# Activation rows placed 64 bytes ahead of the weight rows modulo 256 in a two-block transformer kernel

## The chip, the cores and the metric

The kernel runs on one core of a Trainium2 chip. Its time is device time in microseconds of one launch: 1126.99 us, the median of three runs (1125.65 to 1127.13).

The engines: TensorE (PE) multiplies, its weight loads are listed apart (PEld); VectorE (DVE), ScalarE (ACT) and GpSimd (POOL) do the elementwise work; SyncE (SP) issues the DMAs. PE reads both operands from the on-chip memory SBUF, 128 partitions wide, and writes into PSUM.

## The reference

Two transformer blocks on 256 tokens of width 1024, all in float32. Cut to what matters:

```python
# first block
h = h + 0.5 * swiglu(rmsnorm(h), w_gate, w_up, w_down)        # 1024 -> 2816 -> 1024
n = rmsnorm(h); z = n @ w_in                                  # q, k, v, u, v_gate
attn = causal_attention(q, k, v)                              # 8 heads of 64
gm   = u * (tril(w_s) @ layernorm(gelu(v_gate)) + b_s)        # chunks of 128 tokens
gates = sigmoid(n @ w_gate + b_gate)
h = h + (gates_a * (attn @ w_branch_attn) + gates_g * (gm @ w_branch_gmlp)) @ w_out
h = h + 0.5 * swiglu(rmsnorm(h), ...)
x = rmsnorm(h)
# second block, on 16 meta tokens + 256 tokens = 272
u = rms_norm(h); proj = u @ w_in
y_a = hgrn2_mixer(q, f, i, g) @ w_hg_o      # S_t = diag(f_t) S_{t-1} + k_t v_t^T, o_t = S_t^T q_t
y_b = mla_mixer(c_q, c_kv, k_pe) @ w_mla_o  # latent attention with rope, 8 heads
h = h + rms_norm((gate_a * y_a + gate_b * y_b) @ w_out)
h = h + rms_norm((silu(gt) * up) @ w_ffn_out)
return h[:, 16:, :]
```

## The kernel before

Features lie on partitions and tokens in the columns. A weight matrix is streamed as 168 slabs of up to 1 MB, 2048 float32 words on every partition, through a ring of three places (`RING`, `SLAB`). `stage` receives a slab by DMA. ACT copies it into `w_hi` in the reduced format fp32r (`split_hi`, L1038), DVE writes the rest `stage - w_hi` into `w_lo` (`split_lo`, L1194). Activations are split in the same way into a high and a low part. `x_hi` and `x_lo` hold eight rows (one for each 128 features) of 272 columns: 16 meta tokens and 256 tokens. `a_hi` and `a_lo` hold eight rows of 256.

`products` (L1372) makes one product of two split operands from three matmuls: w_lo with x_hi, w_hi with x_lo, w_hi with x_hi (L1374 to L1376). The first operand is the stationary one, loaded as 128 columns; the second is streamed, 256 or 272 columns wide. Each matmul comes with a load of its own, which PE does beside the matmul before it.

Which operands `products` gets depends on the slab:

- A feature slab (`feature_slab`, L1381) has 8 x 256 columns of weights, stationary in tiles of 128. It streams row k of x or a, for two outputs, k from 0 to 7: 48 matmuls, the row changes every three matmuls. It reads x from column 16 on (`x_hi[:, :, X0:]`). Nine slabs and one half slab of the second mixer (`FULL`, `one_chunk_slab`) read all 272 columns.
- A down slab (`down_slab`, L1423) has 2 x 1024 columns of weights and streams two rows of the hidden activation, 24 matmuls on the first and then 24 on the second (L1429, the last slab of a block interleaves them). `hidden_part` (L185) says where the hidden rows lie: in the first feed-forward block in rows of a, in the second and third in x rows 4 and 5, or 6 and 7, in turn.
- A token slab (`token_slab`, L1518; four in the first mixer) streams the weights past a stationary x. Branch slabs and the slabs of the latent attention work on a.

The program is five stages: feed-forward on x, first mixer, feed-forward on a, second mixer, feed-forward on a. Each engine's instructions stand in a written order, and semaphores tie them. A feed-forward block runs gate, up and down slabs in turn. The mixers put attention, the gating and the decay levels of the recurrence between slabs. At a level (`level`, L639 on DVE and L1703 on PE) PE multiplies 16 pairs of q and k blocks, and DVE copies those elements into `AT` which the level's mask keeps: eight `copy_predicated` (L684) for each of eight levels.

`sb` (L125) gives each tensor the next free bytes of every partition, in the order of the calls. `stage`, `w_hi` and `w_lo` take 24,576 bytes each, then come `x_hi`, `x_lo` (8 x 1088 bytes each), `a_hi`, `a_lo` (8 x 1024), `h`, `sq`, `ar` (all the mixers' scratch), `tab` (mask, cosines, sines and the level masks `lvl`, 128 columns for each of eight levels), `ident` and small things.

Of the kernel before, what the change touches and what calls it, by code (L numbers as in the profile page):

```python
# [20 lines left out]
F32 = mybir.dt.float32  # L21
F32R = mybir.dt.float32r
# [4 lines left out]
P = 128  # L27
D = 1024
DC = D // P
SEQ = 256  # L30
META = 16
L2 = SEQ + META
X0 = META
FF = 2816
PAIRS = FF // 256
# [13 lines left out]
LEVELS = [0, 1, 2, 4, 8, 16, 32, 64]  # L49
# [22 lines left out]


T_MASK, T_COS, T_SIN, T_LVL = 0, L2, 2 * L2, 3 * L2
TAB = T_LVL + P * len(LEVELS)
NEG = -1e30


def constants():


    tab = np.zeros((P, TAB), np.float32)
    q, k = np.arange(P)[:, None], np.arange(P)[None, :]
    tab[:, T_MASK + L2 - P:T_MASK + L2] = np.where(k <= q, 0.0, NEG)
    inv_freq = (1.0 / (np.float32(10000.0) ** (np.arange(0, ROPE, 2, dtype=np.float32) / np.float32(ROPE)))).astype(np.float32)
    ang = (np.arange(L2, dtype=np.float32)[:, None] * inv_freq[None, :]).astype(np.float32)
    row = np.arange(P)
    sign = np.where(row % ROPE < ROPE // 2, -1.0, 1.0).astype(np.float32)
    tab[:, T_COS:T_COS + L2] = np.cos(ang).T[row % (ROPE // 2)]
    tab[:, T_SIN:T_SIN + L2] = np.sin(ang).T[row % (ROPE // 2)] * sign[:, None]  # L90
    s, t = np.arange(P)[:, None], np.arange(P)[None, :]
    for i, h in enumerate(LEVELS):
        keep = (s == t) if h == 0 else ((s // (2 * h) == t // (2 * h)) & (s % (2 * h) < h) & (t % (2 * h) >= h))
        tab[:, T_LVL + P * i:T_LVL + P * i + P] = keep
    return tab


# [24 lines left out]
def program(nc, a, vec_d, id_d, tab_d, out):  # L122
    ctx = ExitStack()
    with ctx:
        def sb(name, shape, dt):  # L125
            return ctx.enter_context(nc.sbuf_tensor(name, shape, dt))

        s = {}
# [6 lines left out]
        stage = sb("stage", [P, RING, SLAB], F32)  # L135
        w_hi = sb("w_hi", [P, RING, SLAB], F32R)
        w_lo = sb("w_lo", [P, RING, SLAB], F32R)
        x_hi = sb("x_hi", [P, DC, L2], F32R)
        x_lo = sb("x_lo", [P, DC, L2], F32R)
        a_hi = sb("a_hi", [P, DC, SEQ], F32R)  # L140
        a_lo = sb("a_lo", [P, DC, SEQ], F32R)
        h = sb("h", [P, DC, SEQ], F32)
        sq = sb("sq", [P, DC, SEQ], F32)
        ar = sb("ar", [P, 17408], F32)
        tab = sb("tab", [P, TAB], F32)
        ident = sb("ident", [P, P], F32)
# [3 lines left out]
        ones = sb("ones", [P, P], F32)  # L150
        eps = sb("eps", [P, 1], F32)
        pick = sb("pick", [P, 2 * HH - 1], F32)
        warm = sb("warm", [P, 16], F32)
        ss = sb("ss", [P, 2, L2], F32)
        std = sb("std", [P, 2, L2], F32)
        rstd = sb("rstd", [P, 2, L2], F32)
        rcol = sb("rcol", [P, 2, 8], F32)

        mask = tab[:, T_MASK:T_MASK + L2]
        lvl = tab[:, T_LVL:].bitcast(mybir.dt.int32).rearrange("p (l t) -> p l t", t=P)  # L160

        def view(at, *dims):
            n = int(np.prod(dims))
# [39 lines left out]
        tA, tB = view(0, 1024), view(1024, 1024)  # L203
        tC, tD = view(11264, 1024), view(12288, 1024)
        meta = sb("meta", [P, 2, DC, META], F32)
        small = sb("small", [P, 96], F32)

        out_tok = view(2048, NT, D)

# [8 lines left out]
        AT = view(13824, HH, 3, P)  # L218
# [375 lines left out]
        def mixer2_dve(dve, split_lo, seq, inverse, input_lo):  # L594
# [44 lines left out]
            def level(l):  # L639


                size = LEVELS[l]
# [31 lines left out]
                    dve.wait_ge(s["lvl_done"], 4 * l)  # L674
                for b in range(4):
                    for hd in range(2):
                        o, m = AT[:, 2 * b + hd, 0:3:2, :], lvl[:, l, :]
                        d = ps[:, 4 + b, SEQ * hd:SEQ * hd + SEQ].rearrange("p (t q) -> p t q", t=2)
                        if size:
                            o, d = (v.rearrange("p t (b two s) -> p t b two s", two=2, s=size)[:, :, :, 1, :] for v in (o, d))  # L680
                            m = m.rearrange("p (b two s) -> p b two s", two=2, s=size)[:, :, 1, :].unsqueeze(1).to_broadcast([P, 2, P // (2 * size), size])
                        else:
                            m = m.unsqueeze(1).to_broadcast([P, 2, P])
                        op = nc.vector.copy_predicated(o, m, d)  # L684
                    op.then_inc(s["lvl_done"], 1)

# [1231 lines left out]
```

## Time and profile before

| | |
|---|---|
| median of 3 runs | 1126.99 us (1125.65 to 1127.13) |
| profiled execution, from first to last instruction | 1125.5 us |
| PE busy | 1098.5 us, 98% |
| PE weight loads busy | 1067.5 us, 95% |
| DVE, ACT, POOL busy | 699.7 (62%), 516.0 (46%), 93.6 us (8%) |
| matmuls recorded | 8807 |
| bytes moved by DMA | 180.19 MB, 160 GB/s on average |

The times come from one profiled execution. A matmul's duration in a row is its way through a pipeline in which several are under way, so the sum of durations is longer than the time they take. How fast they follow each other is seen in the start times of the timeline (first column, in us from the span's start), or in a stretch's length over the count in brackets. PEclk is the share of PE's full clock of 2.4 GHz that was granted; 0.5 is its lower level of 1.2 GHz.

### The profile page before, as it was taken

Reading aid. Unit: us, or ns where it says so; the run is one execution under the profiler, and the core shown is the slowest. Engines: PE = TensorE matmul, PEld = TensorE weight load, DVE = VectorE, ACT = ScalarE, POOL = GpSimd, SP = SyncE. Lnnn points to the kernel's source line nnn. Section 1 sums busy time; section 2 is a strip of 40 time slices with the busy share of each in tenths; the row PEclk is TensorE's granted clock in tenths of the full one; section 3 lists DMA queues with packets and bytes.
Section 4 is the critical chain, followed back from the end, with each engine's and each line's share of the span. In section 5 each row is a group of like instructions: output and inputs, shape, how many; then the busy total and the mean of one; then the engine's idle time right before and its main releaser. Section 6 shows DMA issues by size and latency. Waiting matters only on the chain.

```text
span 1125.5 us, 20359 instructions
## 1 busy us (share of the span) xinstructions
PE 1098.5 (98%) x8807; PEld 1067.5 (95%) x8807; DVE 699.7 (62%) x698; ACT 516.0 (46%) x558; POOL 93.6 (8%) x90
## 2 busy tenths in 40 slices
PE   6999999999999999999999999999999989999997
PEld 5999999999999999999989888999979989999997
DVE  4755555666858665555689666676636656655552
ACT  5543343535755553343375555322333555444334
POOL 3000000100201200000025700000000021000001
PEclk8999999999999999999999999989998989999999
DMA  8466555465354465555436432423323454555541
GB/s 283 141 224 224 181 189 189 138 199 187 115 185 159 151 215 186 188 185 186 149 109 220 149 113 75 143 84 113 113 85 117 137 187 134 209 196 170 186 149 38
DMA packets 147192, 180.19 MB, mean 160 GB/s; under 512 B 3965, under 2 KB 134258, under 8 KB 147138
## 3 DMA queue, kind: packets, MB, share of 16 engines
q1 hardware_dynamic: 146464, 177.55, 48.3%
q0 software_dynamic: 400, 1.73, 0.5%
q8 instruction: 42, 0.69, 0.2%
q10 hardware_dynamic: 274, 0.13, 0.0%
q14 instruction: 12, 0.10, 0.0%
HBM read 178.34 MB, written 1.05 MB: 159 GB/s over the span
## 4 chain that ended last, share of the span: by engine, by line
PE 93%; DVE 3%; issue 2%; ACT 1%; POOL 1%; DVEq 0%; POOLq 0%; ACTq 0%
PE ps L1374 28%; PE ps L1376 27%; PE ps L1375 27%; PE ps L1720 2%; DVE w_lo L1194 1%; PE ps L1678 1%; PE ps L1677 1%; ACT w_hi L1038 1%; PE ps L1759 0%; PE ps L1700 0%; POOL ss L932 0%; PE ps L1757 0%; PE ps L1842 0%; PE ps L1698 0%; PE ps L1738 0%
## 5 line engine op out<-in xcount | busy, mean ns | idle before, releaser
L1194 DVE TENSOR_TENSOR w_lo<-stage,w_hi 128x2048 fp32r<-128x2048 f32 (+1 forms) x165 | 381.4, 2315 | 213.3 <-ACT w_hi L1038 212.9
L1374 PE MATMUL ps<-x_hi,w_lo 128*128 128x256 f32 (+1 forms) x1480 | 422.9, 286 | 4.7 <-DVE ar L703 2.0
L1376 PE MATMUL ps<-x_hi,w_hi 128*128 128x256 f32 (+1 forms) x1480 | 419.6, 284 | 0.0
L1375 PE MATMUL ps<-x_lo,w_hi 128*128 128x256 f32 (+1 forms) x1480 | 419.5, 283 | 0.0
L1038 ACT ACTIVATE w_hi<-stage 128x2048 fp32r<-128x2048 f32 (+1 forms) x165 | 313.2, 1902 | 222.5 <-PE ps L1376 222.5
L1374 PE MATMUL ps<-a_hi,w_lo 128*128 128x256 f32 (+1 forms) x1112 | 316.9, 285 | 2.8 <-DVE a_lo L1200 2.3
L1376 PE MATMUL ps<-a_hi,w_hi 128*128 128x256 f32 (+1 forms) x1112 | 315.8, 284 | 0.0
L1375 PE MATMUL ps<-a_lo,w_hi 128*128 128x256 f32 (+1 forms) x1112 | 315.8, 284 | 0.0
L1374 PEld LDWEIGHTS ps<-x_hi,w_lo 128*128 128x128 f32 x1480 | 282.9, 191 | 10.8 <-issue 7.5
L1376 PEld LDWEIGHTS ps<-x_hi,w_hi 128*128 128x128 f32 x1480 | 282.7, 191 | 0.0
L1375 PEld LDWEIGHTS ps<-x_lo,w_hi 128*128 128x128 f32 x1480 | 282.0, 191 | 0.0
L1374 PEld LDWEIGHTS ps<-a_hi,w_lo 128*128 128x128 f32 x1112 | 214.4, 193 | 3.5 <-issue 3.0
L1375 PEld LDWEIGHTS ps<-a_lo,w_hi 128*128 128x128 f32 x1112 | 214.6, 193 | 0.1
L1376 PEld LDWEIGHTS ps<-a_hi,w_hi 128*128 128x128 f32 x1112 | 214.4, 193 | 0.0
L1065 ACT ACTIVATE ar<-ar 128x512 f32<-128x512 f32 x33 | 20.8, 631 | 121.5 <-DVE ar L1217 121.5
L928 POOL TENSOR_TENSOR ss<-sq 128x256 f32<-128x256 f32 x7 | 6.5, 925 | 759.7 <-ACT sq L1041 391.3
L1074 ACT ACTIVATE x_hi<-ar 128x512 fp32r<-128x512 f32 x22 | 13.9, 632 | 86.6 <-DVE ar L1229 86.6
L1217 DVE TENSOR_TENSOR ar<-ps,rstd 128x512 f32<-128x512 f32 x33 | 22.8, 690 | 34.4 <-PE ps L1376 34.3
L932 POOL TENSOR_TENSOR ss<-ss,sq 128x256 f32<-128x256 f32 x36 | 31.4, 871 | 28.8 <-ACT sq L1041 18.0
L1720 PE MATMUL ps<-ar 128*128 128x64 f32 (+1 forms) x256 | 30.5, 278 | 1.1 <-DVE ar L684 1.1
L1720 PEld LDWEIGHTS ps<-ar 128*128 128x128 f32 x256 | 30.1, 196 | 1.3 <-issue 1.3
L1074 ACT ACTIVATE a_hi<-ar 128x512 fp32r<-128x512 f32 x11 | 6.9, 632 | 45.8 <-DVE ar L1229 45.8
(292 smaller groups left out, 846.8 us busy)
## 6 DMA issues: line engine op xcount, KB each, us to landing
stage<-in_w_in_dram SPq DMA_DIRECT2D x36, 1024.0 KB, 5.2
stage<-in_ffn_w_up_dram SPq DMA_DIRECT2D x22, 1024.0 KB, 5.4
stage<-in_ffn_w_down_dram SPq DMA_DIRECT2D x22, 1024.0 KB, 5.0
stage<-in_w_ffn_in_dram SPq DMA_DIRECT2D x22, 1024.0 KB, 5.0
stage<-in_ffn_w_gate_dram SPq DMA_DIRECT2D x21, 1024.0 KB, 5.3
stage<-in_w_ffn_out_dram SPq DMA_DIRECT2D x11, 1024.0 KB, 4.9
stage<-in_w_gate_dram SPq DMA_DIRECT2D x8, 1024.0 KB, 5.5
stage<-in_w_out_dram SPq DMA_DIRECT2D x8, 1024.0 KB, 5.1
```

Source lines behind the costliest of these rows:

```text
L932: last = nc.gpsimd.tensor_tensor(dst, dst, src[:, c, :], ALU.add)
L1038: nc.scalar.activation(o, i, ACT.Copy).then_inc(s["hi_ready"], 1)
L1065: nc.scalar.activation(ga_a, ga_s, ACT.Silu).then_inc(s["silu_done"], 1)
L1074: nc.scalar.activation(hidden_part(f, 0, J), pair(hid), ACT.Copy).then_inc(s["hid_hi_done"], 1)
L1194: nc.vector.tensor_tensor(o, i, b.bitcast(F32), ALU.subtract).then_inc(s["lo_ready"], 1)
L1217: nc.vector.tensor_tensor(pair(ga_s), ps[:, g0:g0 + 2, 0:SEQ] if first else pair(ps[:, J % 2, :]), bc2, ALU.mult).then_inc(s["gate_scaled" ...
L1374: nc.tensor.matmul(o, wl, xh, start=start, stop=False, skip_group_check=skip)
L1375: nc.tensor.matmul(o, wh, xl, start=False, stop=False, skip_group_check=skip)
L1376: return nc.tensor.matmul(o, wh, xh, start=False, stop=stop, skip_group_check=skip)
L1677: nc.tensor.matmul(o, qn[:, hd, t:t + P], kn[:, hd, 0:nk], start=True, stop=False)
L1678: last = nc.tensor.matmul(o, q_pe[r:r + ROPE, p, t:t + P], k_pe[r:r + ROPE, 0:nk], start=False, stop=True)
L1720: last = nc.tensor.matmul(o, k2[:, hd, X0 + P * t:X0 + P * t + P], q, start=True, stop=True)
```

## The change

The rows of `x_hi` and `x_lo` are allocated 320 columns wide (`X_ROW`), 1280 bytes in place of 1088; the kernel still uses the first 272. `small` (384 bytes) is allocated ahead of `x_hi` and `warm` (64 bytes) between `x_lo` and `a_hi`; both stood further back. The level masks hold only the columns that their level can keep, 64 for each of seven levels, one after the other. Level 0, the diagonal, takes `ident` as its mask. The table shrinks from 1840 to 1264 columns. Counted from the first byte of `stage`, modulo 256:

| begins at | before | after |
|---|---|---|
| weight rows and their tiles of 128 columns | 0 | 0 |
| x row k, column 16 on | 64 (k + 1) | 192 |
| x row k, all 272 columns | 64 k | 128 |
| a rows | 0 | 192 |
| h, sq, ar | 0 | 192 |
| ident | 192 | 128 |

The order and number of instructions is the same on every engine, and so is what each waits for. Two forms differ: the eight masked copies of level 0 read `ident`, and the table's DMA is 128 x 1264 words in place of 128 x 1840.

```diff
@@ -30,6 +30,7 @@
 SEQ = 256
 META = 16
 L2 = SEQ + META
+X_ROW = 320
 X0 = META
 FF = 2816
 PAIRS = FF // 256
@@ -72,7 +73,7 @@
 
 
 T_MASK, T_COS, T_SIN, T_LVL = 0, L2, 2 * L2, 3 * L2
-TAB = T_LVL + P * len(LEVELS)
+TAB = T_LVL + P // 2 * (len(LEVELS) - 1)
 NEG = -1e30
 
 
@@ -89,9 +90,9 @@
     tab[:, T_COS:T_COS + L2] = np.cos(ang).T[row % (ROPE // 2)]
     tab[:, T_SIN:T_SIN + L2] = np.sin(ang).T[row % (ROPE // 2)] * sign[:, None]
     s, t = np.arange(P)[:, None], np.arange(P)[None, :]
-    for i, h in enumerate(LEVELS):
-        keep = (s == t) if h == 0 else ((s // (2 * h) == t // (2 * h)) & (s % (2 * h) < h) & (t % (2 * h) >= h))
-        tab[:, T_LVL + P * i:T_LVL + P * i + P] = keep
+    for i, h in enumerate(LEVELS[1:]):
+        keep = (s // (2 * h) == t // (2 * h)) & (s % (2 * h) < h) & (t % (2 * h) >= h)
+        tab[:, T_LVL + P // 2 * i:T_LVL + P // 2 * (i + 1)] = keep.reshape(P, -1, 2, h)[:, :, 1].reshape(P, P // 2)
     return tab
 
 
@@ -135,8 +136,11 @@
         stage = sb("stage", [P, RING, SLAB], F32)
         w_hi = sb("w_hi", [P, RING, SLAB], F32R)
         w_lo = sb("w_lo", [P, RING, SLAB], F32R)
-        x_hi = sb("x_hi", [P, DC, L2], F32R)
-        x_lo = sb("x_lo", [P, DC, L2], F32R)
+
+        small = sb("small", [P, 96], F32)
+        x_hi = sb("x_hi", [P, DC, X_ROW], F32R)[:, :, 0:L2]
+        x_lo = sb("x_lo", [P, DC, X_ROW], F32R)[:, :, 0:L2]
+        warm = sb("warm", [P, 16], F32)
         a_hi = sb("a_hi", [P, DC, SEQ], F32R)
         a_lo = sb("a_lo", [P, DC, SEQ], F32R)
         h = sb("h", [P, DC, SEQ], F32)
@@ -150,14 +154,13 @@
         ones = sb("ones", [P, P], F32)
         eps = sb("eps", [P, 1], F32)
         pick = sb("pick", [P, 2 * HH - 1], F32)
-        warm = sb("warm", [P, 16], F32)
         ss = sb("ss", [P, 2, L2], F32)
         std = sb("std", [P, 2, L2], F32)
         rstd = sb("rstd", [P, 2, L2], F32)
         rcol = sb("rcol", [P, 2, 8], F32)
 
         mask = tab[:, T_MASK:T_MASK + L2]
-        lvl = tab[:, T_LVL:].bitcast(mybir.dt.int32).rearrange("p (l t) -> p l t", t=P)
+        lvl = tab[:, T_LVL:].bitcast(mybir.dt.int32).rearrange("p (l t) -> p l t", t=P // 2)
 
         def view(at, *dims):
             n = int(np.prod(dims))
@@ -203,7 +206,6 @@
         tA, tB = view(0, 1024), view(1024, 1024)
         tC, tD = view(11264, 1024), view(12288, 1024)
         meta = sb("meta", [P, 2, DC, META], F32)
-        small = sb("small", [P, 96], F32)
 
         out_tok = view(2048, NT, D)
 
@@ -674,13 +676,13 @@
                     dve.wait_ge(s["lvl_done"], 4 * l)
                 for b in range(4):
                     for hd in range(2):
-                        o, m = AT[:, 2 * b + hd, 0:3:2, :], lvl[:, l, :]
+                        o = AT[:, 2 * b + hd, 0:3:2, :]
                         d = ps[:, 4 + b, SEQ * hd:SEQ * hd + SEQ].rearrange("p (t q) -> p t q", t=2)
                         if size:
                             o, d = (v.rearrange("p t (b two s) -> p t b two s", two=2, s=size)[:, :, :, 1, :] for v in (o, d))
-                            m = m.rearrange("p (b two s) -> p b two s", two=2, s=size)[:, :, 1, :].unsqueeze(1).to_broadcast([P, 2, P // (2 * size), size])
+                            m = lvl[:, l - 1, :].rearrange("p (b s) -> p b s", s=size).unsqueeze(1).to_broadcast([P, 2, P // (2 * size), size])
                         else:
-                            m = m.unsqueeze(1).to_broadcast([P, 2, P])
+                            m = ident[:].bitcast(mybir.dt.int32).unsqueeze(1).to_broadcast([P, 2, P])
                         op = nc.vector.copy_predicated(o, m, d)
                     op.then_inc(s["lvl_done"], 1)
```

## Rows read from the trace of the kernel before

**Rows 1.** The page, parts 1, 2 and 4 (busy time and share; GB/s in 40 slices; chain)

```profile
PE 1098.5 (98%) x8807; PEld 1067.5 (95%) x8807; DVE 699.7 (62%) x698; ACT 516.0 (46%) x558; POOL 93.6 (8%) x90
...
GB/s 283 141 224 224 181 189 189 138 199 187 115 185 159 151 215 186 188 185 186 149 109 220 149 113 75 143 84 113 113 85 117 137 187 134 209 196 170 186 149 38
...
PE ps L1374 28%; PE ps L1376 27%; PE ps L1375 27%; PE ps L1720 2%; DVE w_lo L1194 1%; PE ps L1678 1%; PE ps L1677 1%; ACT w_hi L1038 1%; PE ps L1759 0%; PE ps L1700 0%; POOL ss L932 0%; PE ps L1757 0%; PE ps L1842 0%; PE ps L1698 0%; PE ps L1738 0%
```

**Rows 2.** PE's waits: line, releaser, us in total, times, longest

```profile
PE ps L1720 <- DVE ar L684: 1.1, 1, 1.1
```

**Rows 3.** PE's groups by form: line, op, tiles, form, count | busy us, mean ns

```profile
L1374 PE MATMUL ps<-x_hi,w_lo 128*128 128x256 f32 x1328 | 377.0, 284 | 4.7 <-DVE ar L703 2.0 <-DVE x_lo L1200 0.9 <-issue 0.9
...
L1374 PE MATMUL ps<-a_hi,w_lo 128*128 128x256 f32 x1096 | 312.2, 285 | 2.6 <-DVE a_lo L1200 2.3 <-issue 0.4
...
L1374 PE MATMUL ps<-x_hi,w_lo 128*128 128x272 f32 x152 | 45.9, 302 | 0.0
```

**Rows 4.** Timeline of PE (start us, us), x and a in steady slabs

```profile
67.46 0.28 PE L1374 MATMUL ps<-x_hi,w_lo 128*128 128x256 f32 x1
...
78.83 0.28 PE L1374 MATMUL ps<-a_hi,w_lo 128*128 128x256 f32 x1
...
457.14 0.28 PE L1374 MATMUL ps<-a_hi,w_lo 128*128 128x256 f32 x1
...
463.26 0.28 PE L1374 MATMUL ps<-a_hi,w_lo 128*128 128x256 f32 x1
```

**Rows 5.** Timeline of PE, one down slab on x rows 6 and 7

```profile
467.33 0.28 PE L1375 MATMUL ps<-x_lo,w_hi 128*128 128x256 f32 x1
...
469.37 0.28 PE L1375 MATMUL ps<-x_lo,w_hi 128*128 128x256 f32 x1
...
470.18 0.28 PE L1376 MATMUL ps<-x_hi,w_hi 128*128 128x256 f32 x1
...
472.34 0.28 PE L1376 MATMUL ps<-x_hi,w_hi 128*128 128x256 f32 x1
```

**Rows 6.** Timeline of PE, one down slab on x rows 4 and 5

```profile
450.14 0.28 PE L1375 MATMUL ps<-x_lo,w_hi 128*128 128x256 f32 x1
...
452.38 0.28 PE L1376 MATMUL ps<-x_hi,w_hi 128*128 128x256 f32 x1
...
452.97 0.28 PE L1375 MATMUL ps<-x_lo,w_hi 128*128 128x256 f32 x1
...
455.23 0.28 PE L1376 MATMUL ps<-x_hi,w_hi 128*128 128x256 f32 x1
```

**Rows 7.** Timeline of PE, a slab that reads 272 columns

```profile
641.01 0.29 PE L1375 MATMUL ps<-x_lo,w_hi 128*128 128x272 f32 x1
...
644.04 0.29 PE L1375 MATMUL ps<-x_lo,w_hi 128*128 128x272 f32 x1
```

**Rows 8.** Stretches: us, then PE, PEld, DVE, ACT, POOL busy, PEclk, DMA, GB/s

```profile
30.00:210.00 180.00, 180.00 (x1516) 179.96 (x1515) 108.40 (x89) 75.35 (x59) 0.00 (x0) 1.00 0.57 189
363.00:563.00 200.00, 200.00 (x1680) 199.95 (x1680) 119.30 (x92) 87.48 (x72) 6.24 (x7) 1.00 0.56 183
937.00:1110.00 173.00, 173.00 (x1456) 173.00 (x1455) 99.62 (x75) 71.73 (x56) 0.00 (x0) 1.00 0.50 167
563.00:716.00 153.00, 149.39 (x1049) 134.01 (x1048) 109.42 (x144) 86.59 (x129) 45.17 (x37) 0.99 0.43 136
716.00:920.00 204.00, 201.19 (x1557) 191.59 (x1556) 124.90 (x155) 76.73 (x77) 4.54 (x5) 0.97 0.38 122
736.00:744.00 8.00, 8.00 (x43) 8.00 (x43) 6.48 (x10) 0.00 (x0) 0.00 (x0) 0.57 0.40 133
```

**Rows 9.** Groups by line on DVE, the hidden part's second half

```profile
L1232 DVE TENSOR_TENSOR x_lo<-ar,x_hi 128x512 fp32r<-128x512 f32 x22 | 15.2, 693 | 17.6 <-ACT x_hi L1074 17.6
...
L1232 DVE TENSOR_TENSOR a_lo<-ar,a_hi 128x512 fp32r<-128x512 f32 x11 | 7.6, 692 | 8.8 <-ACT a_hi L1074 8.8
```

**Rows 10.** One line's instructions: ns min/median/max, DVE's masked copies

```profile
L684 DVE COPY_PREDICATED ar<-tab,ps x64: 284/295/504, 720.3 to 802.2; 128x128 f32<-128x128 int32 x56, 128x256 f32<-128x256 int32 x8
```

## Prediction

> **What bounds the kernel now.** I read the page first. PE is busy 98% of the 1125.5 us span, and the heaviest lines of the chain that ended last are the three matmuls of `products` with 28, 27 and 27% [rows 1]. PE idles 1125.5 - 1098.5 = 27 us in all, most of it at the start, at the norms between stages and at the end; of the waits for other engines inside a stage the largest is 1.1 us, for DVE's masked copies [rows 2]. So the time is the number of matmuls times the time from one matmul's start to the next. The means of 282 to 302 ns in [rows 3] are whole flights through a pipeline and tell nothing of that pace. It is read from the starts in the timeline, or from a window's length over its count.
>
> The count, by form [rows 3]: 3 x 1328 = 3984 matmuls stream 256 columns of x, 3 x 1096 = 3288 stream 256 columns of a, 3 x 152 = 456 stream 272 columns of x. In four token slabs (192 matmuls) and in two half slabs of kv x or a is the stationary side.
>
> The pace differs by buffer. In the first feed-forward block 96 matmuls on x take 78.83 - 67.46 = 11.37 us, 118.4 ns each; on a 51 gaps take 6.12 us, 120.0 ns each [rows 4]. Whole blocks agree: 180.00 us / 1516 = 118.7, 200 / 1680 = 119.0, 173 / 1456 = 118.8 ns [rows 8]. In these windows PE never idles and the clock is at its full level of 2.4 GHz, at which 256 columns are 106.7 ns. So 12 to 13 ns of each matmul is something else.
>
> **The experiment that the trace already holds.** The weight rows (`w_hi`, `w_lo`, each 24,576 bytes = 96 x 256) all begin at one residue modulo 256, and so does every 128-column tile of them (512 bytes apart). Call how far past it an activation row begins, modulo 256, its offset. Before, x rows of 1088 = 4 x 256 + 64 bytes, read from token 16 (64 bytes on), have the offsets 64 (k + 1): 64, 128, 192, 0 for rows 0 to 3 and again for rows 4 to 7. a rows are all at 0. A feature slab changes its x row every three matmuls, so no offset can settle. But the down slabs of the second and third feed-forward blocks hold one x row for 24 matmuls (`hidden_part`, rows 4 and 5 or 6 and 7), with everything else the same:
> - row 6, offset 192: 18 gaps take 469.37 - 467.33 = 2.04 us, 113.3 ns each [rows 5]
> - row 7, offset 0: 18 gaps take 472.34 - 470.18 = 2.16 us, 120.0 ns, exactly a's pace [rows 5]
> - row 4, offset 64: 19 gaps take 2.24 us, 117.9 ns [rows 6]
> - row 5, offset 128: 19 gaps take 2.26 us, 118.9 ns [rows 6]
>
> In cycles of 2.4 GHz that is 272 against 288 for 256 columns. Ten such slabs with rows 6 and 7 stand in the trace, five in each block, all alike. Offset 192 is 64 bytes ahead of the weight rows, and it settles within four or five matmuls from a's pace.
>
> The page "TensorE: Matmul & The Clock Gate" of the Trainium skill says otherwise, in "Step-by-step: what each phase is for": the array has two independent read ports, and "Loading the next tile's weights doesn't steal SBUF read bandwidth from the running matmul." By that rule the place of a row would change nothing and the sum would be zero. The trace disagrees: 113.3 against 120.0 ns with the row's place as the only difference [rows 5]. Its result is rival 3.
>
> **The change, part by part.** Each engine gets the instructions it had, in their order, with the same waits; only addresses, the mask's shape and one DMA's size change.
>
> *Rows of x.* `small` (384 = 256 + 128 bytes) now stands ahead of `x_hi`, and a row is 320 x 4 = 1280 = 5 x 256 bytes. Read from token 16 every row is at 128 + 64 = 192; `x_lo`, 10,240 = 40 x 256 bytes on, too. `hidden_part` uses the same rows. Of the 3984 matmuls the 20 down slabs (960) stand now at 113.3, 120.0, 117.9 and 118.9 in equal parts: 240 x (0 + 6.7 + 4.6 + 5.6) ns = 4.1 us. The other 3024 go from 118.4, the nearest long row, to 113.3: 15.4 us.
>
> *Rows of a.* `warm` (64 bytes) ahead of `a_hi` brings a's rows of 1024 bytes to 192 as well: 3288 x (120.0 - 113.3) = 22.0 us.
>
> *Sum of both:* 41.5 us. To be taken off: matmuls in the stretches at the lower clock level, where the window of 8 us holds 43 at a mean clock of 0.57 [rows 8] and the pace is set by the 1.2 GHz clock; there are four such stretches and one at the start, some 110 matmuls x 5.5 ns = 0.6 us. The first four or five matmuls after each change of pattern or wait, and feature slabs that run below 118.4 just after a wait: about 1 us. That leaves 40 us.
>
> *Reads of 272 columns* start 64 bytes earlier in the row and so all stand at 128. Now they mix all four offsets, 24 gaps in 3.03 us, 126.3 ns [rows 7]. Row 5's offset is 118.9 against a mean of (117.9 + 118.9 + 113.3 + 120.0) / 4 = 117.5, so +1.4 ns x 456 = +0.6 us. Bounds: as at 192, -4.2 x 456 = -1.9; as at 0, +2.5 x 456 = +1.1. I take +0.6.
>
> *Token slabs.* The stationary rows are at 192 and the streamed weights at 0, so the streamed side begins 64 past the other, as row 4 does, at 117.9. I take no change; bounds for 192 matmuls at 113.3 or 120.0 against 118.4: -1.0 and +0.3 us.
>
> *Everything behind x moves.* `h`, `sq`, `ar` and `ident` keep their distances modulo 256 from each other and from a, so matmuls within `ar` and the transposes see nothing. DVE does not feel where x lies: the subtraction of 512 elements takes 693 ns on x rows at all offsets and 692 on a rows at 0 [rows 9]. Zero, bounds those of one ns in 692.
>
> *Masks.* 56 masked copies read a contiguous mask in place of a strided one, 8 read `ident`. The 64 copies take 284 to 504 ns, median 295 [rows 10], and PE waits for them once, 1.1 us [rows 2]. If 56 fell from 295 to 284 ns DVE would save 0.6 us; if all took the 504 of the widest it would lose 11.7 us over seven levels, of which PE's slabs hide most: -0.6 to +3 us. I take 0, the median's side. The table is 0.29 MB smaller, loaded early behind other work: 0.
>
> *What is late next.* In the feed-forward blocks nothing: three slabs take 17.1 us now and 16.3 then, DVE is busy 119.3 and ACT 87.5 of 200 us [rows 8], and 190 us still hold both; the weights stream at 183 GB/s [rows 8] and would need 192, where the first slice of the page moved 283 [rows 1]. In the mixers DVE is busy 109.4 of 153 us and 124.9 of 204 [rows 8], and at the decay levels its chain is as long as PE's slab, which is why the 1.1 us wait is there. There a 256-column slab of 48 matmuls shrinks from 5.7 to 5.4 us and DVE's part does not; for five such slabs around the levels I give back 1.5 us, with 0 and 11 us (all that the two mixers would gain, rival 1) as bounds. Waits at the norms are chains of DVE, ACT and POOL and stay.
>
> *Total:* 41.5 - 1.6 - 0.6 - 1.5 = 37.8 us, say 38. The profiled span is 1125.5 us, 1.5 below the median of 1126.99 and at the low end of its runs (1125.65); from the median the forecast is 1089 us.
>
> **Rivals.**
> 1. *The mixers gain nothing.* DVE takes over there as the bound. For it: the 1.1 us wait and DVE at 109.4 of 153 us from 563 to 716. Against it: PE never idles for long there though DVE has slack. By block, the gain of 1516, 1680 and 1456 matmuls down to 113.3 ns is 8.2 + 9.6 + 8.0 = 25.8 us; the ends of the blocks add about 1. Time: 1100.
> 2. *The period is longer than 256 bytes* (512, say). Every second x row would miss the offset of row 6. Half of x's 19.5 us is lost: 1127 - 28 = 1099. Against it: rows k and k + 4 lie 4352 = 17 x 256 bytes apart, an odd multiple, and feature slabs on x show no difference between them; a rows sit as row 6 does modulo 1024.
> 3. *Placement does nothing*, and 113.3 is row 6's by some other cause. 1127. Against it: ten of ten slabs.
> 4. *Slower: a standing offset is itself the cost.* PE's load and stream fall into step when the row's place doesn't change, as on a (120.0), and x's changing rows are what has kept it at 118.4. Then a stays and x goes to 120: 3984 x 2.0 = +8 us, 1135. It decides where the settled pace at 192 in feature slabs is over the 119 ns of today's mean; that pace is not in the trace, since a feature slab never holds 192 for more than three matmuls. For it: a and row 7 do lock at the slowest pace. Against it: row 6 locks at 113.3 for 20 matmuls while weights advance as in a feature slab.
> 5. *More than forecast:* the lower clock stretches shift or vanish. The one in the window of 8 us costs (1 - 0.57) x 8 = 3.4 us [rows 8]. Two gone and the good end of the 272 reads: 1081.
>
> **How the numbers follow.** Forecast 0.80, with its own range 1084 to 1096 (40 us full gain plus one clock stretch fewer; 4 us more given back plus one stretch more). Rival 1 0.06, rival 2 0.03, rival 3 0.04, rival 4 0.03, rival 5 0.04. The range for 8 in 10 takes in rivals 1, 2 and 5 and leaves out 3 and 4: 1081 to 1101. A change under 0.2% (2.3 us) can't be told from none. Faster: 0.80 + 0.06 + 0.03 + 0.04 = 0.93. Same: rival 3, 0.04. Slower: rival 4, 0.03.
>
> **What would show it.** Right: matmul starts 113.3 ns apart in gate, up and down slabs alike, on x and on a; 144 matmuls in 16.3 us; the 272 reads near 127 ns; DVE's and ACT's mean times as before. Wrong at the first step: 118 or 120 ns anywhere in a steady slab on 256 columns, every second row slow (rival 2), or 120 throughout (rival 4). Wrong at the last step: a pace of 113.3 but new idle time of PE in the mixers, behind DVE (rival 1).

## The result, and the profile after

The changed kernel took 1106.3 us, the median of four runs (1104.8 to 1108.9), against 1126.3 for the kernel before beside it: ratio 0.983 (95% interval 0.981 to 0.986). The gain is 20 us where 38 were forecast, and 1106 lies outside the range of 1081 to 1101.

The page of the kernel after, the two parts that answer to [rows 1] (line numbers are 2 higher than before):

```profile
PE 1079.7 (98%) x8807; PEld 1047.9 (95%) x8807; DVE 698.3 (63%) x698; ACT 516.2 (47%) x558; POOL 93.0 (8%) x90
...
PE ps L1376 27%; PE ps L1377 26%; PE ps L1378 26%; PE ps L1722 2%; ACT w_hi L1040 1%; PE ps L1680 1%; PE ps L1679 1%; DVE w_lo L1196 1%; ACT ar L340 1%; DMA stage<-in_ffn_w_gate_dram 0%; PE ps L1761 0%; PE ps L1702 0%; POOL ss L934 0%; PE ps L1759 0%; DVE ar L686 0%
```

PE idles 1107.2 - 1079.7 = 27.5 us, as before (27). DVE and ACT are busy as long as before. So nothing was handed to another engine; PE's own pace is not what was forecast. Three stretches inside the three feed-forward blocks show it, with the columns of [rows 8]:

```profile
75.00:203.00 128.00, 128.00 (x1132) 128.00 (x1131) 76.65 (x57) 54.55 (x40) 0.00 (x0) 1.00 0.60 202
405.00:545.00 140.00, 140.00 (x1191) 140.00 (x1190) 81.03 (x61) 56.78 (x42) 0.00 (x0) 1.00 0.57 185
948.00:1074.00 126.00, 126.00 (x1072) 126.00 (x1071) 73.97 (x54) 50.81 (x39) 0.00 (x0) 1.00 0.57 190
```

The first block is as forecast: 128.00 / 1132 = 113.1 ns. The other two are not: 117.5 ns each (single starts there lie 117.8 apart; a count over a window is rough by one or two). Offsets and clock are the same in all three. The first block's gate and up slabs stream x and its down slabs a, and the other two blocks have it the other way round, but in the third block a runs at 113.3 too, until 931 us. The timeline of PE there (start us, us) shows the change of pace:

```profile
930.88 0.28 PE L1376 MATMUL ps<-a_hi,w_lo 128*128 128x256 f32 x1
930.99 0.28 PE L1377 MATMUL ps<-a_lo,w_hi 128*128 128x256 f32 x1
931.10 0.28 PE L1378 MATMUL ps<-a_hi,w_hi 128*128 128x256 f32 x1
931.53 0.38 PE L1376 MATMUL ps<-x_hi,w_lo 128*128 128x256 f32 x1 [0.15 <-DVE w_lo L1196]
931.75 0.28 PE L1377 MATMUL ps<-x_lo,w_hi 128*128 128x256 f32 x1
931.87 0.28 PE L1378 MATMUL ps<-x_hi,w_hi 128*128 128x256 f32 x1
931.98 0.28 PE L1376 MATMUL ps<-x_hi,w_lo 128*128 128x256 f32 x1
```

Before the short wait for DVE's half of the weights the starts are 0.11 us apart, behind it 0.12 (in the trace's full digits 113, 113, 114 and then 118, 118, 118, 117). The slow pace then lasts, over gate, up and down slabs, to the end of the block 160 us later. So offset 192 has two settled paces, 113.3 and 117.8 ns (272 and nearly 283 cycles of 2.4 GHz), and a wait can leave either.

One measure serves for all runs: take the gaps between starts of successive 256 column matmuls of `products` that stream the same buffer, leave out those of 130 ns and more (waits, the 1.2 GHz stretches), and sum what each has over 113.33 ns (272 cycles). I call it the excess. It is 39.7 us before and 19.3 after, over about 7230 gaps each. By stage:

| excess, us | ff 1 | mixer 1 | ff 2 | mixer 2 | ff 3 |
|---|---|---|---|---|---|
| before | 8.7 | 5.0 | 9.8 | 7.2 | 8.9 |
| after | 0.0 | 0.7 | 7.6 | 4.9 | 6.1 |

### The profile page after: what moved, and what is told of

Its sections match the earlier page's. It is cut to its first block, busy times and chain, and to the rows that moved or that the text cites. A ratio compares the mean times of both kernels' runs of the same rounds, so it can differ in the third digit from the quotient of the medians.

```text
span 1107.2 us, 20359 instructions
## 1 busy us (share of the span) xinstructions
PE 1079.7 (98%) x8807; PEld 1047.9 (95%) x8807; DVE 698.3 (63%) x698; ACT 516.2 (47%) x558; POOL 93.0 (8%) x90
## 4 chain that ended last, share of the span: by engine, by line
PE 89%; DVE 4%; ACT 4%; issue 1%; POOL 1%; DMA 0%; DVEq 0%; SPq 0%; ACTq 0%; POOLq 0%
PE ps L1376 27%; PE ps L1377 26%; PE ps L1378 26%; PE ps L1722 2%; ACT w_hi L1040 1%; PE ps L1680 1%; PE ps L1679 1%; DVE w_lo L1196 1%; ACT ar L340 1%; DMA stage<-in_ffn_w_gate_dram 0%; PE ps L1761 0%; PE ps L1702 0%; POOL ss L934 0%; PE ps L1759 0%; DVE ar L686 0%
## 5 line engine op out<-in xcount | busy, mean ns | idle before, releaser
L1376 PE MATMUL ps<-a_hi,w_lo 128*128 128x256 f32 (+1 forms) x1112 | 313.7, 282 | 3.1 <-DVE a_lo L1202 2.2
L1377 PE MATMUL ps<-a_lo,w_hi 128*128 128x256 f32 (+1 forms) x1112 | 312.3, 281 | 0.0
L1378 PE MATMUL ps<-a_hi,w_hi 128*128 128x256 f32 (+1 forms) x1112 | 312.3, 281 | 0.0
L1376 PEld LDWEIGHTS ps<-a_hi,w_lo 128*128 128x128 f32 x1112 | 211.9, 191 | 4.4 <-issue 3.1
L1378 PEld LDWEIGHTS ps<-a_hi,w_hi 128*128 128x128 f32 x1112 | 211.5, 190 | 0.0
L1377 PEld LDWEIGHTS ps<-a_lo,w_hi 128*128 128x128 f32 x1112 | 210.3, 189 | 0.1
```

The lines of the kernel that those rows point to most:

```text
L1376: nc.tensor.matmul(o, wl, xh, start=start, stop=False, skip_group_check=skip)
L1377: nc.tensor.matmul(o, wh, xl, start=False, stop=False, skip_group_check=skip)
L1378: return nc.tensor.matmul(o, wh, xh, start=False, stop=stop, skip_group_check=skip)
```

## The experiments

Each series ran beside the kernel before on one chip, five chips in all; its medians there were 1123.6 to 1125.6 us. Theory A: two settled paces at offset 192, chosen at a disturbance. The rivals: the second and third block are slow for a reason of their own, such as traffic (B), or x rows are fast and a rows slow wherever they lie (C). In what follows a draw is what happens at a wait: the stretch behind it settles at one pace or the other.

**x alone, a alone.** e2 adds 64 bytes ahead of `a_hi` to the changed kernel (a back at offset 0); e3 adds 192 bytes ahead of `a_hi` to the kernel before. Whatever stands behind `a_hi` moves along in both.

```diff
+        pad = sb("pad", [P, 16], F32)     # e2, in the changed kernel
+        pad = sb("pad", [P, 48], F32)     # e3, in the kernel before
         a_hi = sb("a_hi", [P, DC, SEQ], F32R)
```

> The changed kernel with 64 more bytes ahead of a_hi: x rows at offset 192, a rows at 0 as before. Theory A (offset 192 has two settled paces, 113.3 and 117.8 ns; the first matmuls after a wait choose; coming from a's settled 120.0 the choice is always 113.3): every down slab of the second and third feed-forward block, which comes from a at 120.0, runs at 113.3 on both rows, and the first block on x at 113.3 or 117.8 as a whole. Time 1127 - 4.1 (down slabs) - 5.4 (first block, if fast) - 3 to 7 (mixers) = 1110 to 1115 us. Theory B (the second and third block are slow for a reason of their own, such as other engines' or the DMAs' traffic there): their down slabs stand at 117.8, time 1116 or more. Theory C (x rows are fast in any place, a rows slow in any place): down slabs at 113.3 too, but then a_only brings nothing.

> The kernel before with 192 bytes of padding ahead of a_hi: a rows at offset 192, x rows and masks as before. Theory A: the gate slab behind each down slab that ended on row 7 (offset 0, settled at 120.0) and the up slab behind it run at 113.3; those behind row 5 (offset 128) run at 113.3 or 117.8. 3288 matmuls on a gain between 2.2 and 6.7 ns: 7 to 22 us, 1105 to 1120, and about 1108 if half of the slabs behind row 5 are fast. Theory B (the second and third block are slow for a reason of their own): all gate and up slabs there at 117.8, first block's down slabs at 113.3: 1127 - 7.2 - 2.4 = 1117 us. Theory C: a stays slow, 1120 or more.

e2: 1110.8 us, ratio 0.987 (0.985 to 0.988). e3: 1105.3 us, ratio 0.982 (0.980 to 0.984). The timeline of e2, a gate slab on a at 120.0 that ends, a down slab on x that begins, and the same slab 18 gaps later:

```profile
424.38 0.28 PE L1378 MATMUL ps<-a_lo,w_hi 128*128 128x256 f32 x1
424.50 0.28 PE L1379 MATMUL ps<-a_hi,w_hi 128*128 128x256 f32 x1
424.62 0.29 PE L1377 MATMUL ps<-x_hi,w_lo 128*128 128x256 f32 x1
424.74 0.28 PE L1378 MATMUL ps<-x_lo,w_hi 128*128 128x256 f32 x1
...
425.20 0.28 PE L1379 MATMUL ps<-x_hi,w_hi 128*128 128x256 f32 x1
...
427.25 0.28 PE L1379 MATMUL ps<-x_hi,w_hi 128*128 128x256 f32 x1
```

(427.25 - 425.20) / 18 = 113.9 by the rounded rows, 113.3 in full digits, and so do all 16 such slabs of the second and third block that I read, both rows. In e3 it is a that runs at 113.3: 2906 of its 3220 gaps are 113 or 114 ns, 1823 of 1989 in those two blocks. e2's down slabs are against B, and a in e3 is against C. In both kernels the offset changes at every down slab. One entry of e3 came out otherwise: behind the down slab at 931 us a starts at 117.8, without a wait, and keeps it for 96 matmuls, across a wait; behind the next down slab, at 954 us, it is back at 113.3. Each part works alone, and the two gains add to 15 + 20 = 35 us, more than both together gave in the first series, and near the 32.6 us that they gave on this chip (e4, next).

**The changed kernel again.** Five more series of the same file.

> The changed kernel once more, for a second profile. If the choice between 113.3 and 117.8 ns after a wait is drawn anew in each execution, the first, second and third block come out differently from the first profile (fast, slow, slow), and the runs spread by 8 us and more. If the program's own timing fixes it, the same stretches are fast and slow, and the time is 1105 to 1109 us again.

> The changed kernel a third time, beside e5_seed. If the choice of pace differs between loads of the program or between chips, its median lies anywhere from 1091 to 1109 us, and the block that is slow is told by its starts: 144 matmuls of a gate, an up and a down slab take 16.96 us at 117.8 ns and 16.32 us at 113.3. If the first profile was the exception, 1091 to 1098 us.

> The changed kernel a fourth time, the control for the other three. Its runs should fall into groups by how many of the two blocks (second and third feed-forward) are slow: none near 1092, one near 1099, both near 1106 us, since 1450 matmuls x 4.5 ns = 6.5 us is one block. Times spread evenly between 1092 and 1109 would speak against whole blocks being the unit.

> The changed kernel a fifth time, as control beside e13_kick and e15_seed_again. By the waits that end each block's start it lies at 1092, 1099 or 1106 us, and its profile shows the whole rest of a block at the pace that the last wait chose.

> The changed kernel a sixth time, as control: 1092, 1099 or 1106 us by the number of blocks that a wait has left at 117.8 ns. Over its profiles so far, span minus what the 256 column matmuls take beyond 113.3 ns each is 1084 to 1089 us; the same is expected here.

Medians 1093.1, 1093.5, 1106.9, 1094.7 and 1099.1 us; with the first series 32 runs from 1091.0 to 1108.9, and 13 of them above 1103. So one and the same program has two answers 14 us apart, and the interval of the first series (0.981 to 0.986) held for that series only; e4's is 0.969 to 0.975. The same three stretches in e4:

```profile
75.00:203.00 128.00, 128.00 (x1132) 128.00 (x1131) 76.84 (x58) 54.44 (x40) 0.00 (x0) 1.00 0.61 202
405.00:545.00 140.00, 140.00 (x1238) 140.00 (x1237) 84.75 (x63) 58.72 (x43) 0.00 (x0) 1.00 0.59 189
948.00:1074.00 126.00, 126.00 (x1114) 126.00 (x1114) 72.88 (x55) 50.74 (x38) 0.00 (x0) 1.00 0.53 175
```

1238 in place of 1191: both blocks fast. In e17 it is the first and the third block that stand at 117.8:

```profile
75.00:203.00 128.00, 128.00 (x1089) 128.00 (x1089) 72.49 (x54) 52.26 (x39) 0.00 (x0) 1.00 0.57 191
405.00:545.00 140.00, 140.00 (x1235) 140.00 (x1236) 83.66 (x62) 59.04 (x44) 0.00 (x0) 1.00 0.60 197
```

Where they part is seen at one place, the start of an up slab near 399 us, where PE meets DVE. First the changed kernel's first profile, then e4:

```profile
398.82 0.28 PE L1378 MATMUL ps<-a_hi,w_hi 128*128 128x256 f32 x1
399.01 0.39 PE L1376 MATMUL ps<-a_hi,w_lo 128*128 128x256 f32 x1
399.23 0.28 PE L1377 MATMUL ps<-a_lo,w_hi 128*128 128x256 f32 x1
399.35 0.28 PE L1378 MATMUL ps<-a_hi,w_hi 128*128 128x256 f32 x1
399.46 0.28 PE L1376 MATMUL ps<-a_hi,w_lo 128*128 128x256 f32 x1
399.58 0.28 PE L1377 MATMUL ps<-a_lo,w_hi 128*128 128x256 f32 x1
399.70 0.28 PE L1378 MATMUL ps<-a_hi,w_hi 128*128 128x256 f32 x1
399.82 0.28 PE L1376 MATMUL ps<-a_hi,w_lo 128*128 128x256 f32 x1
```

```profile
398.79 0.28 PE L1378 MATMUL ps<-a_hi,w_hi 128*128 128x256 f32 x1
398.99 0.39 PE L1376 MATMUL ps<-a_hi,w_lo 128*128 128x256 f32 x1
399.21 0.28 PE L1377 MATMUL ps<-a_lo,w_hi 128*128 128x256 f32 x1
399.33 0.28 PE L1378 MATMUL ps<-a_hi,w_hi 128*128 128x256 f32 x1
399.45 0.28 PE L1376 MATMUL ps<-a_hi,w_lo 128*128 128x256 f32 x1
399.56 0.28 PE L1377 MATMUL ps<-a_lo,w_hi 128*128 128x256 f32 x1
399.68 0.28 PE L1378 MATMUL ps<-a_hi,w_hi 128*128 128x256 f32 x1
399.79 0.28 PE L1376 MATMUL ps<-a_hi,w_lo 128*128 128x256 f32 x1
```

Both were slow before the wait. The gaps behind it are 225, 115, 118, 117, 118 ns in the first and 221, 120, 117, 116, 114, 113 in the second: an entry differs by a few ns and one block of about 1300 matmuls follows it, 1300 x 4.5 = 5.9 us. Over the two profiles, a stretch of 24 or more gaps on one buffer that begins behind a wait or a 1.2 GHz stretch settled at the fast pace 42 times and at the slow one 37 times. In the six profiles of this kernel the pace never changed inside a stretch at offset 192 without a wait. Span against excess, over all profiles of the changed kernel:

| | span | excess | difference |
|---|---|---|---|
| after | 1107.2 | 19.3 | 1087.9 |
| e12 | 1106.3 | 17.5 | 1088.8 |
| e17 | 1104.3 | 16.0 | 1088.3 |
| e6 | 1097.2 | 10.8 | 1086.4 |
| e14 | 1093.7 | 9.3 | 1084.4 |
| e4 | 1091.6 | 6.1 | 1085.5 |

The difference is level within 4.4 us and the excess spans 13.2: the pace explains nearly all of what parts these runs. e17 lies where its expectation has it (1084 to 1089). My groups of 1092, 1099 and 1106 were too clean. The first block and the mixers draw too, and runs lie between (1097.7, 1103.4).

**A disturbance at every slab.** e9 splits one matmul of each 256 column feature slab:

```diff
+ nc.tensor.matmul(o, wl_, src[0][:, 0, :], start=True, stop=False)
+ nc.tensor.matmul(o[:, 0:P], wh_, src[1][:, 0, 0:P], start=False, stop=False)
+ nc.tensor.matmul(o[:, P:], wh_, src[1][:, 0, P:], start=False, stop=False)
+ nc.tensor.matmul(o, wh_, src[0][:, 0, :], start=False, stop=False)
```

> The changed kernel, with the second matmul of every 256 column feature slab split into two of 128 columns: a small disturbance at the start of some 95 slabs, with no change of offset and no wait. It costs about 60 ns each, 5 to 6 us. Rival A2 (each disturbance is a draw between 113.3 and 117.8): the pace differs from slab to slab inside the feed-forward blocks, with about half the slabs slow: 1092 + 6 + 10 = about 1108 us. Theory A1 (any disturbance frees the engine from 117.8 and it ends at 113.3): all gate and up slabs fast, 1096 to 1099 us. Third possibility (only a wait that drains the engine chooses, short disturbances are absorbed): whole blocks fast or slow as in the changed kernel, 1098 to 1112.

1106.3 us. By the time alone that is where rival A2 and the third possibility have it too; the pace decides. The excess is 4.8 us, the lowest of all, beside a control (e12) with 17.5: of 134 stretches without a wait in front 125 run at 113.3. Seven of the 103 splits stand in a stretch at 117.8 with no wait over 0.05 us beside them, and all seven leave it at 113.3. One, at 885 us, was entered at 113.3 and left at 117.8, and seven that stood right behind a wait did not prevent 117.8. But a split costs 0.11 us, not 0.06 (the gaps are 113, 57, 113, 170 where 113, 113, 113 stood), and 103 of them take back 12 us. The pace is nearly A1's (a disturbance frees, though not every time); my price was half of the true one.

**Two cheap disturbances.** e5 (run again as e15) puts row 4 of every second down slab of the later blocks at offset 0. e13 (again as e16) makes the split in ten up slabs only.

```diff
+            if f > 0 and J % 2 == 0:                                            # e5, in hidden_part
+                at, row = 4 * X_ROW + X0 + 16, X_ROW - 16
+                return xf[part][:, at:at + 2 * row].rearrange("p (c t) -> p c t", t=row)[:, :, 0:SEQ]
-                    feature_slab(m, halves(2 + J % 2), ffn_input(f), it=it)
+                    feature_slab(m, halves(2 + J % 2), ffn_input(f), it=it, kick=f > 0 and J == J0 + 2)   # e13
```

> The changed kernel, but in the second and third feed-forward block every second down slab streams its first hidden row (row 4) from 64 bytes further on, offset 0; row 5, rows 6 and 7 and everything else stay at 192. Theory A1 (the pace of 117.8 at offset 192 lasts only because nothing disturbs it; a change of the row's offset shakes the engine loose, and it then settles at 113.3): from the first such down slab on, both blocks run at 113.3 except for the 11 rows at offset 0, which cost 24 x (116.7 to 120.0 - 113.3) ns each, 0.9 to 1.8 us in all. Time 1088 to 1093 us whatever the changed kernel shows on the same chip, and less spread. Rival A2 (the choice is a draw at every disturbance, an offset change included): about half of the slabs at 117.8, 1095 to 1106 us, as the changed kernel.

> The changed kernel with the small disturbance of e9_split (one matmul split in two of 128 columns) in one of 144 x 2 matmuls only: in the middle of the second up slab of every loop iteration of the second and third feed-forward block, ten times in all. Each costs 0.115 us, 1.2 us together. Theory A1: from the first of them on both blocks run at 113.3 ns whatever the waits before chose, so the time is 1092 + 1.2 = 1093 us, with mixers and entries adding up to 4: 1092 to 1097, also where the changed kernel beside it is at 1106. Rival (the split frees the engine only when repeated at every slab, as in e9_split): times like those of the changed kernel, plus 1.

> e5_seed once more, beside e13_kick and the control. Theory A1: the disturbance by an offset does the same as the split and costs 0.6 us more in all (11 x 0.16 = 1.8 against 1.2): 1093 to 1098 us, below the control where the control has a slow block, above it by about 2 where it has none.

> e13_kick once more, since in its first series the control had no slow runs but one. Theory A1: 1091 to 1100 us wherever it runs. If the control is near 1106 here and this stays below 1100, the slow pace is the cause of the difference; if it follows the control to 1107, the cause is something else that goes with it.

In e13 both blocks run at 113.3 in the stretches below:

```profile
405.00:545.00 140.00, 140.00 (x1238) 140.00 (x1237) 84.32 (x62) 58.79 (x43) 0.00 (x0) 1.00 0.58 188
948.00:1074.00 126.00, 126.00 (x1114) 126.00 (x1113) 74.36 (x55) 50.71 (x38) 0.00 (x0) 1.00 0.53 175
```

But that profile doesn't show a split at work: each of its ten splits was entered at 113.3 already, the first (403 us) behind a wait that had left the fast pace. e16 holds the one that was needed, at 938.7 us. Twelve gaps in front of it, the split, twelve gaps behind it:

```profile
937.02 0.28 PE L1378 MATMUL ps<-a_hi,w_hi 128*128 128x256 f32 x1
...
938.43 0.28 PE L1378 MATMUL ps<-a_hi,w_hi 128*128 128x256 f32 x1
938.55 0.28 PE L1404 MATMUL ps<-a_hi,w_lo 128*128 128x256 f32 x1
938.67 0.22 PE L1405 MATMUL ps<-a_lo,w_hi 128*128 128x128 f32 x1
938.73 0.27 PE L1406 MATMUL ps<-a_lo,w_hi 128*128 128x128 f32 x1
938.84 0.33 PE L1407 MATMUL ps<-a_hi,w_hi 128*128 128x256 f32 x1
...
939.24 0.28 PE L1378 MATMUL ps<-a_hi,w_hi 128*128 128x256 f32 x1
...
940.60 0.28 PE L1378 MATMUL ps<-a_hi,w_hi 128*128 128x256 f32 x1
```

1.41 / 12 = 117.5 ns before, 1.36 / 12 = 113.3 behind, and the rest of the block stays there. In the first profile the same block, left at 117.8 by its wait, stayed slow to its end.

The runs of one series each, sorted; the first three rows share a chip, the last two another:

| | us |
|---|---|
| e13 | 1091.3, 1094.8, 1095.2, 1096.2, 1099.5, 1100.4 |
| e15 | 1092.2, 1092.7, 1095.6, 1095.7, 1102.5, 1102.7 |
| e14, control | 1091.0, 1093.9, 1094.0, 1095.4, 1095.9, 1105.3 |
| e16 | 1091.0, 1095.0, 1096.6, 1096.7, 1097.2, 1098.2 |
| e17, control | 1092.3, 1096.1, 1097.7, 1100.5, 1106.1, 1108.6 |

e5 took 1093.7 to 1098.9 us, median 1096.5, beside e6, the control, with 1093.5: its expectation, 1088 to 1093, was missed, and it was no better than its control. In its profile and in e15's both later blocks are fast (excess 6.6 and 5.6 us), but no row at offset 0 was entered at 117.8 there, so they don't show that it frees.

Of 12 runs of the kernel with ten splits none is above 1100.4, of 12 runs of its control three are above 1105, and of all 32 of the changed kernel 13 above 1103. That agrees with A1, but is weak by itself: none of 12 against three of 12 can be chance, two series of the changed kernel (e4, e6) have none above 1103 either, and only one run of each series has a profile. What carries A1 are the eight splits entered at 117.8, in e9 and e16, all of them left at 113.3, and the table of span against excess. What I promised besides, a time of 1092 to 1098 throughout, is missed by four of e15's and e13's twelve runs. Those four have no profile; whether a mixer, the first block or the clock made them is open. As a version to keep the ten splits are worth little: the slowest of their 12 runs is 8 us below the slowest of the 32 without, if that isn't chance, and they cost 1.1 us where the draw was good (median 1096.4 of 12 runs, against 1098.4 of 32).

**Other offsets.** e7 makes `small` 64 bytes wider, so that all rows stand at 0. e10 puts 64 bytes ahead of `w_hi`, so that weights and activations move together. e1 moves everything from `x_hi` on in the kernel before by 32 bytes. e11 moves x alone there by 16: its rows begin four words into a larger allocation (a multiple of 256 bytes larger, so a keeps its offset).

```diff
-        small = sb("small", [P, 96], F32)
+        small = sb("small", [P, 112], F32)    # e7
+        pad = sb("pad", [P, 16], F32)         # e10, ahead of w_hi
+        pad = sb("pad", [P, 8], F32)          # e1, ahead of x_hi
```

> The changed kernel with small 64 bytes wider: all activation rows, of x and of a, at offset 0 in place of 192 (and the 272 column reads at 192 in place of 128). If the common offset sets the pace, x and a run at 120.0 or 116.7 ns, the two paces that offset 0 has shown (in before and in e1_shift32), never at 113.3: 7272 matmuls x (120.0 - 119.0) = +7 us over before, or x (116.7 - 119.0) = -17 us: 1110 to 1134 us. If uniform placement by itself was the gain and not its value, 1091 to 1106 us.

> The changed kernel with 64 bytes of padding ahead of w_hi: weights and activations both move by 64 bytes, the distance between them stays at 192. If only the distance counts, 113.3 and 117.8 ns are again the only settled paces and the time is that of the changed kernel on the same chip (1091 to 1109 us). If the absolute place counts, other paces appear (116.7, 118.9, 120.0) and the time goes toward 1118 to 1135 us.

> The kernel before with 32 bytes of padding ahead of x_hi, nothing else. The x rows read from token 16 then begin at 96, 160, 224 and 32 past the weight rows (rows 4, 5, 6, 7 of the down slabs in the second and third feed-forward block); a stays at 0. It shows the pace of four offsets that neither kernel has. If the pace depends on the offset in steps of 64 bytes, each of the four equals one neighbour of 120.0, 117.9, 118.9, 113.3 ns. If 113.3 is a narrow optimum at 192, rows 6 (224) and 5 (160) stand at 116 to 119. If only the row's identity counts and not its place, row 6 stays at 113.3 and row 7 at 120.0. Time within 3 us of before in each case.

> The kernel before with x 16 bytes further on: rows 4 to 7 begin at 80, 144, 208 and 16 past the weight rows. It shows how wide the good place at 192 is. If it is a matter of the 64 byte step, 208 (row 6, entered from a's pace as before) stays at 113.3 ns; if it is narrow, as 160 and 224 suggest (118 to 120 in e1_shift32), row 6 lies between 115 and 119. Time 1118 to 1128 us.

e7: 1128.9 us, ratio 1.006 (1.004 to 1.008), slower than before. Every 256 column slab on x and a stands at 120.0:

```profile
405.00:545.00 140.00, 140.00 (x1169) 140.00 (x1169) 81.34 (x61) 56.61 (x42) 0.00 (x0) 1.00 0.58 190
```

So it is the value of the offset that gains, not uniformity; with the wrong value uniform rows lose 5 us, by the medians. The excess is 48.2 us against 39.7, and the 272 column reads, now at 192, give 1.4 us back. The Trainium skill says in "TensorE: Matmul & The Clock Gate", "Step-by-step: what each phase is for", that loading weights takes no read bandwidth from the running matmul. Between e7 and e6, which ran side by side and differ by 64 bytes of padding, lie 35 us, so for these pairs of load and matmul the place of the streamed rows does matter; no run tells whether read bandwidth is what it costs.

e10: 1096.7 us (1093.5 to 1103.0), again only 113.3 and 117.8 on x and a. For the paces the distance counts, not the place. Whether the place bears on the draw is open: on the same chip none of e10's four runs is above 1103, and all six of the control's (e12) are.

e1: 1120.8 us in its one run. The down slabs settle at 120.0 (offset 96), 118.7 (160), 118.3 (224) and 116.7 (32), and e11, 1126.2 us in its one run, at 119.9 (80), 116.7 (144), 119.5 (208) and 118.7 (16). Row 6 of e11, at 208, 18 gaps:

```profile
433.83 0.28 PE L1376 MATMUL ps<-x_hi,w_hi 128*128 128x256 f32 x1
...
435.98 0.28 PE L1376 MATMUL ps<-x_hi,w_hi 128*128 128x256 f32 x1
```

2.15 / 18 = 119.4 ns. The good place is narrow on this side: 16 bytes beyond 192 cost the whole gain; 176 was not tried. My expectation of e1 has a slip that e7's repeats: a did not stay at 0. `a_hi` stands behind `x_hi`, so the 32 bytes move a as well, to offset 32, and there it runs at 116.7 ns, the pace of row 7 at the same offset. By the excess a gains 10 us in e1 and x loses 3. Offset 0 has shown one pace only, 120.0, in before, e2, e7 and e11 (there a kept its place).

**The masks alone.** The kernel before with `TAB`, `constants` and `level` of the changed one.

> The kernel before with only the level masks compact (64 columns for each of seven levels, ident for level 0); all tensors ahead of the table where they were, those behind it 2304 = 9 x 256 bytes earlier, so at the same place modulo 256. My sum has 0 for it, bounds -0.6 to +3 us. If the masks take back part of the gain, 1128 to 1132 us; the mean of the 64 masked copies by shape (284, 295, 504 ns) tells which.

1125.6 against 1123.6 us, ratio 1.001 (0.999 to 1.003): nothing that can be measured. In the kernel after, the 56 copies take what they took [rows 10], and the 8 of level 0 take 434 ns where they took 441 (the 504 of [rows 10] are narrower ones; the changed kernel has them too, at 509):

```profile
L686 DVE COPY_PREDICATED ar<-tab,ps x56: 283/294/509, 718.6 to 786.2; 128x128 f32<-128x128 int32 x56
L686 DVE COPY_PREDICATED ar<-ident,ps x8: 431/434/443, 707.3 to 709.6; 128x256 f32<-128x256 int32 x8
```

## Why the prediction was wrong

The step that failed is the one in which row 6's pace became the pace of offset 192: "it settles within four or five matmuls from a's pace" [rows 5], and the two terms built on it, 15.4 us for x and 22.0 for a. The observation was right, and it was ten times the same observation. Every one of those slabs was entered from a at 120.0, without a wait, after a change of offset. In e2 such entries give 113.3 too, all of them; in e3, where a is entered from x, all but one. What the changed kernel makes is another thing, long stretches at 192 entered from a wait, of which the trace before holds none; there it is a draw between 113.3 and 117.8. The change also took away what keeps a stretch short: before, the row's offset changed every few matmuls or at each down slab. That such a change frees the engine rests on e2, on e3 (954 us) and on the first mixer of the changed kernel, where feature slabs on x follow a token slab at 117.8 and fall to 113.3 without a wait (between 240 and 249 us, in all six profiles).

Point by point:

- *Rows of x and of a.* Expected 41.5 us less 1.6. Measured by the excess: x 17.6 to 8.5, a 21.2 to 10.4, weights streamed 0.9 to 0.4; 20.4 us in all. In e4, where the draws fell well, 39.7 - 6.1 = 33.6. The terms were nearly right as the best case (x had 17.6 to give where 19.5 stood in the sum, a 21.2 where 22.0 stood), and wrong as the forecast. The token slabs, taken as unchanged, gained 0.5 us: with x at 192 as the stationary side they too run at 113.3, and behind a wait at 117.8.
- *Reads of 272 columns.* Expected near 127 ns. Below, after and then e7, 24 gaps each: 3.04 / 24 = 126.7 at 128 and 2.96 / 24 = 123.3 at 192. The row was a good guide here.

```profile
640.44 0.29 PE L1376 MATMUL ps<-x_hi,w_lo 128*128 128x272 f32 x1
...
643.48 0.29 PE L1376 MATMUL ps<-x_hi,w_lo 128*128 128x272 f32 x1
```

```profile
643.71 0.28 PE L1376 MATMUL ps<-x_hi,w_lo 128*128 128x272 f32 x1
...
646.67 0.28 PE L1376 MATMUL ps<-x_hi,w_lo 128*128 128x272 f32 x1
```

- *DVE, masks, what moves.* Right: the subtraction takes 692 ns [rows 9], and e8 is level.
- *What is late next.* "In the feed-forward blocks nothing" was wrong in a way that mattered. PE now meets DVE's half of the weights near 399, 931 and 943 us, where the trace before has no such gap. The waits are 0.2 to 0.4 us, 0.8 us together, and they start the draw. The 1.5 us given back in the mixers can't be told from the draws there (4.9 us of excess in the second).
- *The clock.* 97 gaps of 213 ns, the 1.2 GHz level, in the first profile against 70 before: 2.7 us more. That closes the sum: 20.4 gained less 2.7 leaves 17.7, and the spans differ by 1125.5 - 1107.2 = 18.3.
- *The rivals.* 1 and 2 did not happen: PE idles no more in the mixers, and no row stands out against another. 3 fell: e7 and e6 differ by the place alone. 4 came nearest in kind, and I gave it 0.03. It said that a standing offset can lock at a bad pace. That is what happens, at 117.8 in place of 120, and only at some entries. e7 is rival 4 at offset 0, where I had put it; I had priced it at 1135 and it took 1128.9.

What stays open: why a given entry ends at one pace or the other, and why whole series lean to one side (four of four and six of six runs above 1103 in two series, none of four and none of six in two others). Of the changed kernel no two series are on record from the same chip, so chip and loading can't be told apart; the chip alone doesn't decide, as e10 beside e12 shows, unless the shifted place does. e14 and e17 hold fast and slow runs in one series.

## What to carry to other kernels

Where matmuls come one after another with a weight load each, try the distance between streamed and stationary rows modulo 256 in steps of 16 or 32 bytes; here 192 gave 113.3 ns, and 160, 208 and 224 gave 118.3 to 119.5. Before a pace seen in one place is multiplied by a count, ask how the engine got into it in that place, and whether the changed kernel gets in the same way. When a pace can lock, a single series says little: load the program again, elsewhere, and compare profiles by the sum of the gaps before believing an interval of 0.5%.

## What the runs showed of the hardware that I had not expected

- The same matmuls on the same addresses have several steady paces: 113.3 or 117.8 ns at offset 192. They last more than 1000 matmuls without any change. The pace goes by the offset in steps as small as 16 bytes: 120.0 at 0, 118.7 at 16, 116.7 at 32, 113.3 at 192 and 119.5 at 208.
- A stretch leaves the slow pace at offset 192 by a small disturbance: a matmul split in two (eight of eight entered at 117.8 left at 113.3), a row at another offset (e3 at 954 us).
- Splitting a 256 column matmul into two of 128 costs 0.11 us: the starts follow each other after 57, 113 and 170 ns, where two whole matmuls take 227.
- The kernel before is not fixed either: over more than 60 runs it lay between 1119.5 and 1128.1 us.
